# Moving three small buffers, and multiplying constants in four kinds of TensorE waits of the RWKV mixer

## The chip, the cores and the metric

The kernel runs on one core of a Trainium2 chip. The metric is the device time in microseconds (us) of one execution; a run's time is a little longer than the span of the instructions in its profile. TensorE (PE in the profile) multiplies, VectorE (DVE), ScalarE (ACT) and GpSimd (POOL) do the element-wise work, SyncE (SP) issues transfers. The profile also gives TensorE's granted clock, where 1.00 is 2.4 GHz and 0.50 is 1.2 GHz.

## The reference

A backbone of two layers over 256 latent and 256 context tokens of 1024 channels, all in float32. In each layer the modulated rows go through one input projection, which feeds four mixers of 4 heads x 64 channels; their outputs are joined, projected, normed and fed to a gated MLP. The mixer that matters here is RWKV-7, a recurrence over tokens that runs in both directions:

```python
def step(S, xt):
    r_t, w_t, k_t, v_t, a_t, b_t = xt
    sa = jnp.einsum('bhvk,bhk->bhv', S, a_t)
    S = S * w_t[:, :, None, :] + sa[..., None] * b_t[:, :, None, :] + v_t[..., None] * k_t[:, :, None, :]
    return S, jnp.einsum('bhvk,bhk->bhv', S, r_t)
...
for layer in range(DEPTH):
    ...
    y_a = _rwkv7_mixer(...)
    ...
    h = _norm(DEEPNORM_ALPHA * h + mod[2] * y, ln_g[layer, 0], ln_b[layer, 0])
    f = _conv_ffn(_modulate(h, mod[3], mod[4]), ffn_w_up[layer], ...)
```

## The kernel before

The kernel keeps the whole stream in SBUF, channels or tokens on the 128 partitions, and streams the weights in. Each layer is a row of stages, each one a block in which every engine has its own written-out program and waits on semaphores: the input projection with the differential attention, mLSTM, HGRN2, then RWKV (`rwkv`, line 1876, the fourth mixer to be finished), then output projection and MLP (`project_and_feed`). Large float32 products are done as three products of rounded halves (`product`, lines 235 to 237), so weights and rows are split first by ScalarE (line 224) and VectorE (line 228).

SBUF buffers are laid out in the order in which they are made: `const`, `par`, `pr` (34 tiles of 512 columns, and under the name `pr_r` the same memory), `mix` (8 tiles), `modc`, `fcol`, `fold`, `ln2`, `hx`. `pr`, `mix` and `ring` receive weights by transfers; `ring` lies behind `hx`.

The RWKV stage turns the recurrence into products over 4 tiles of 128 tokens (TILES = 4), for direction d = 0 and then d = 1. TensorE's program, in order:

- `turns` (line 1978): transposes of the scaled rows.
- `raw` (line 2022): products of all token pairs of a tile, for the list RAW0. `js` are the tiles whose output is needed: four in layer 0, two in layer 1, so RAW0 has 8 entries in layer 0 and 6 in layer 1. VectorE masks them (`raw_out`, line 2364), GpSimd picks small blocks (line 2277), VectorE reduces them to `diag` (line 2399).
- `solve(d)` (line 2054): 7 products that spread `diag`. VectorE then inverts 8x8 blocks row by row (lines 2413 and 2414) and lays them out (line 2422, semaphore xT). For d = 0 solve(0) comes after the sixth entry of RAW0.
- the loop over j with x0 (line 2074), which waits for xT; then the units u = 0 to 15 with `first` (lines 2089 and 2092) and `second` (lines 2111, 2113 and 2118), which double the size of the inverted blocks, with a copy by ScalarE (line 2596) and one by VectorE (line 2455 or 2461) between them.
- in d = 0, after units 11, 13 and 15 (TURN_AT), the turns for direction 1. The first waits for the semaphore scaled, which VectorE sets at the end of `prepare` (lines 2311 to 2340).
- products P and Q (lines 2145 to 2161), and then the four steps m over the tiles: state products (line 2195), for which VectorE waits (line 2488, semaphore u), and `into_state` (line 2185, semaphore s_mm), for which VectorE waits in line 2504; it then sets s, for which the next step waits.
- in d = 0 solve(1), then the products of y (lines 2228 to 2235).

A helper is there already, and is called with 3 before the first turns and with 2 before the products P of d = 1; its result is read by nobody:

```python
def keep_busy(n, out):
    for _ in range(n):
        nc.tensor.matmul(out, ident, const[:, 0:out.shape[-1]], start=True, stop=True)
```

Of the kernel before, what the change touches and what calls it, by code (L numbers as in the profile page):

```python
# [25 lines left out]
KD = D // P  # L26
SIDE = 256
T = 2 * SIDE
TILES = T // P
# [115 lines left out]
def build(nc, A, out):  # L145
    Stage.zeroed, Stage.made = [], 0
    with ExitStack() as ctx, ExitStack() as between:
        def sb(name, cols):
            return ctx.enter_context(nc.sbuf_tensor(name, [P, cols], F32))

        const = sb("const", N_CONST)
        par = sb("par", N_PAR)
        with nc.sbuf_tensor("pr_r", [P, IN_TILES * T], F32R) as pr_r:
            pass
        pr = sb("pr", IN_TILES * T)
        with nc.sbuf_tensor("mix_r", [P, KD * T], F32R) as mix_r:
            pass
        mix = sb("mix", KD * T)
        modc = sb("modc", DEPTH * 4 * KD * 2)
        fcol = sb("fcol", 16)  # L160
        fold = sb("fold", 2 * KD)
        ln2 = sb("ln2", 2 * KD)
        hx = sb("hx", 2 * D)
        ps = [ctx.enter_context(nc.psum_tensor(f"ps{i}", [P, 512], F32)) for i in range(8)]

        def c(o, n=P, rows=P):
            return const[0:rows, o:o + n]

        ident = c(C_ID)
        stored = ctx.enter_context(nc.semaphore("stored"))  # L170
        E = dict(stored=stored, nc=nc, A=A, out=out, c=c, const=const, ident=ident, par=par, hx=hx, pr=pr, pr_r=pr_r, mix=mix, mix_r=mix_r,
                 modc=modc, fcol=fcol, fold=fold, ln2=ln2, ps=ps)
        for layer in range(DEPTH):
            kept = ExitStack()
            with nc.sbuf_tensor(f"hr0_in{layer}", [P, KD * T], F32R) as hr0, nc.sbuf_tensor(f"hr1_in{layer}", [P, KD * T], F32R) as hr1, \
                    nc.sbuf_tensor(f"wr_in{layer}", [P, 4 * W_IN], F32R) as E["wr"], nc.sbuf_tensor(f"coef{layer}", [P, 20], F32) as E["coef"]:
                E["hr"] = (hr0, hr1)
                with Stage(nc, spans=True) as shared:
                    E["proj"] = Projection(E, shared, layer)
                    if layer == 0:  # L180
                        with nc.sbuf_tensor("hc_in", [P, 2 * D], F32, side="right") as E["hc"]:
                            front(E, layer)
                    else:
                        front(E, layer)
                        between.close()
                    with nc.sbuf_tensor(f"work_in{layer}", [P, 9600], F32) as E["work"]:
                        diff_attention(E, layer)
                    E["cond"] = kept.enter_context(nc.sbuf_tensor(f"cond{layer}", [P, 4 * KD + 32 * KD], F32, side="right"))
                    E["cum"] = hx if layer == 0 else kept.enter_context(nc.sbuf_tensor(f"cum{layer}", [P, 4 * T], F32, side="right"))
                    with nc.sbuf_tensor(f"work_m{layer}", [P, 9600 if layer == 0 else 7952], F32) as E["work"]:  # L190
                        mlstm(E, layer)
            with nc.sbuf_tensor(f"gate_r{layer}", [P, 2 * len(sides(layer)) * D], F32R) as E["gate_r"]:
                pass
            with nc.sbuf_tensor(f"gate{layer}", [P, 2 * len(sides(layer)) * D], F32) as E["gate"]:
                with nc.sbuf_tensor(f"work_r{layer}", [P, 13312], F32R) as E["work_r"], \
                        nc.sbuf_tensor(f"ring_r{layer}", [P, 4096], F32R) as E["ring_r"]:
                    pass
                with nc.sbuf_tensor(f"work{layer}", [P, 13312], F32) as E["work"], \
                        nc.sbuf_tensor(f"ring{layer}", [P, 4096], F32) as E["ring"]:
                    hgrn(E, layer)  # L200
                    with Stage(nc, spans=True) as E["out_sems"]:
                        rwkv(E, layer)
                        kept.close()
                        if layer == 0:
                            E["hc"] = between.enter_context(nc.sbuf_tensor("hc", [P, 2 * D], F32, side="right"))
                        project_and_feed(E, layer)
# [1669 lines left out]
def rwkv(E, layer):  # L1876
# [74 lines left out]
    with Stage(nc) as S, nc.Block() as block:  # L1951
        for n in ("link", "tT", "raw", "raw_out", "masks", "t1", "t1_out", "x_up", "d_mm", "u_mm", "s_mm", "u", "s"):
            S(n)
        fcol = E["fcol"]
# [47 lines left out]
        def _(pe):  # L2002
# [45 lines left out]
            pe.wait_ge(S("tT_out"), 2)  # L2048
            def solve(d):

                pe.wait_ge(S("pick"), 1)
                pe.wait_ge(S("diag"), TILES * (d + 1))
                for n, (s_, _) in enumerate(step_rows(d)):
                    mm = nc.tensor.matmul(spread_row(n), pick[:, s_ * P:(s_ + 1) * P], diag, start=True, stop=True)
                mm.then_inc(S("spread"), 1)
# [9 lines left out]
            for d in range(2):  # L2065
                alT, beT, kT, U, rr_ = alTs[d], beTs[d], kTs[d], Us[d], rrs[d]

                for j in range(TILES):
                    pe.wait_ge(S("xT"), TILES * d + j + 1)
                    if j >= 2:  # L2070
                        pe.wait_ge(S("x_up"), (NU + TILES) * d + j - 1)
                    for hd in range(HEADS):
                        for h in range(2):
                            mm = nc.tensor.matmul(ps[2 + j % 2][rows_of(h), hd * HALF:(hd + 1) * HALF], small(j, 0, hd)[rows_of(h)],
                                                     ident[rows_of(h), rows_of(h)], start=True, stop=True)
                    mm.then_inc(S("x0"), 1)
# [44 lines left out]
                for u in range(NU + 1):  # L2121
                    if u < NU:
                        first(u)
                    if u >= 1:
                        second(u - 1)
                    if d == 1 and u in RAW_AT:
                        raw_next(TILES + RAW_AT.index(u))
                    if d == 0 and u in TURN_AT:
                        r = TURN_AT.index(u)
                        if r == 0:  # L2130
                            pe.wait_ge(S("scaled"), 2)
                        else:
                            pe.wait_ge(S("turned1_out"), r)
                        turns((al, be, ks)[r], (6, 7)).then_inc(S("turned1"), 1)
# [45 lines left out]
                def into_state(j, lh, rh, first_):  # L2180

                    for i in range(2):
                        for q in range(2):
                            a = j * 256 + (2 * i + q) * HD
                            mm = nc.tensor.matmul(ps[2][q * HD:(q + 1) * HD, i * HD:(i + 1) * HD], lh[:, a:a + HD], rh[:, a:a + HD],
                                                  start=first_ and i == 0, stop=not first_ and i == 1)
                    return mm

                pe.wait_ge(S("q_a"), d + 1)
                for m, j in enumerate(ORDER[d]):  # L2190
                    if m:
                        pe.wait_ge(S("s"), (TILES - 1) * d + m)
                        for i in range(2):
                            for q in range(2):
                                mm = nc.tensor.matmul(ps[q][:, i * HD:(i + 1) * HD], PT[q * HD:(q + 1) * HD, i * T + j * P:i * T + (j + 1) * P],
                                                      st[q * HD:(q + 1) * HD, (2 * j + i) * HD:(2 * j + i + 1) * HD], start=True, stop=True)
                        mm.then_inc(S("u_mm"), 1)
                    if m < TILES - 1:
                        into_state(j, kT, vT, True)
                    if d == 0 and m == 1:  # L2200
                        raw_next(3)
                    if d and m in (1, 2):
                        gate(m - 1, True)
                    if d and m == 3:
                        bonus_sum(1)
                    if m:
                        pe.wait_ge(S("u"), (TILES - 1) * d + m)
                    if m < TILES - 1:
                        into_state(j, beT, U if m else Q, False).then_inc(S("s_mm"), 1)
                    if d == 0 and m == 0:  # L2210
                        raw_next(2)
                    if d and m < 2:
                        gate(m, False)
                    if d and m == 2:
                        pe.wait_ge(S("q_b"), 2)
                        bonus_sum(0)
# [1131 lines left out]
```

## Time and profile before

| | |
|---|---|
| median of 3 runs | 1829.49 us (1824.72 to 1830.16) |
| the profiled execution | 1827.64 us |
| its span | 1825.7 us |
| mean granted clock | 0.931 |
| TensorE, VectorE, ScalarE, GpSimd busy | 1636.0, 1090.6, 637.4, 82.9 us |

Busy time of TensorE is the union of its multiplies, whose ends are modelled; a busy TensorE at half the clock does half the work. The share of the whole span says little of a stage of some 100 us, so the rows below are taken from the RWKV stages alone.

### The profile page before, as it was taken

What the parts mean: (1) busy time and instruction counts of PE and PEld (TensorE: products, weight loads), DVE (VectorE), ACT (ScalarE), POOL (GpSimd) and SP (SyncE); (2) the same over time, 40 slices, a digit from 0 to 9 for tenths busy, and PEclk for the clock granted to TensorE, in tenths of its full rate; (3) what the DMA queues carried; (4) which work ended last, traced back from release to release, by engine and by line L of the source; (5) the groups of instructions that cost most, each with busy time, mean ns of one, the idle gap of its engine ahead of it and who ended that gap; (6) DMA issues with size and microseconds to landing.
All of it is one profiled execution on the core that took longest, in us unless ns stands there. A gap on an engine that the chain in (4) does not pass through costs nothing. (4 is left out here: it accounts for less than half of the span.)

```text
span 1825.7 us, 29434 instructions
## 1 busy us (share of the span) xinstructions
PE 1636.0 (90%) x12112; PEld 1284.3 (70%) x12112; DVE 1090.6 (60%) x1870; ACT 637.4 (35%) x1060; POOL 82.9 (5%) x112
## 2 busy tenths in 40 slices
PE   6999999789778999999999979999977688989996
PEld 4766767565477778888877757678754487668875
DVE  2285346885775674554442254735786757578765
ACT  4254221433321245222232242433344231356651
POOL 0000011300201000000000000000120200000000
PEclk8999899899788999999999989999979698989998
DMA  9311111265201034222222022212232201245550
GB/s 391 124 46 47 58 58 58 92 232 186 94 3 48 25 139 154 100 92 93 92 93 92 1 85 81 70 47 81 70 119 92 94 3 48 97 185 188 188 197 23
DMA packets 41620, 182.01 MB, mean 100 GB/s; under 512 B 4752, under 2 KB 5520, under 8 KB 33680
## 3 DMA queue, kind: packets, MB, share of 16 engines
q1 hardware_dynamic: 41488, 180.14, 27.7%
q8 instruction: 96, 1.57, 0.4%
q14 instruction: 36, 0.29, 0.0%
HBM read 179.08 MB, written 1.05 MB: 99 GB/s over the span
## 5 line engine op out<-in xcount | busy, mean ns | idle before, releaser
L235 PE MATMUL ps<-hr_in,wr_in 128*128 128x512 f32 (+1 forms) x544 | 222.0, 408 | 14.4 <-DVE wr_in L228 12.3
L236 PE MATMUL ps<-hr_in,wr_in 128*128 128x512 f32 (+1 forms) x544 | 209.0, 384 | 0.0
L237 PE MATMUL ps<-hr_in,wr_in 128*128 128x512 f32 (+1 forms) x544 | 208.6, 383 | 0.0
L235 PEld LDWEIGHTS ps<-hr_in,wr_in 128*128 128x128 f32 x544 | 108.6, 200 | 65.4 <-issue 36.5
L228 DVE TENSOR_TENSOR wr_in<-mix,wr_in 128x1024 fp32r<-128x1024 f32 x68 | 83.9, 1235 | 93.9 <-ACT wr_in L224 93.5
L235 PE MATMUL ps<-mix_r,work_r 128*128 128x512 f32 (+1 forms) x352 | 136.3, 387 | 1.6 <-DVE work_r L228 1.6
L236 PE MATMUL ps<-work_r 128*128 128x512 f32 (+1 forms) x356 | 135.6, 381 | 0.0
L228 DVE TENSOR_TENSOR work_r<-pr,work_r 128x2048 fp32r<-128x2048 f32 x38 | 87.0, 2289 | 72.1 <-ACT work_r L224 68.0
L237 PE MATMUL ps<-mix_r,work_r 128*128 128x512 f32 x320 | 127.2, 397 | 0.0
L2907 PE MATMUL ps<-mix_r,work_r 128*128 128x512 f32 x336 | 120.7, 401 | 2.3 <-DVE mix_r L228 2.3
L237 PEld LDWEIGHTS ps<-hr_in,wr_in 128*128 128x128 f32 x544 | 108.2, 199 | 19.8
L236 PEld LDWEIGHTS ps<-hr_in,wr_in 128*128 128x128 f32 x544 | 108.7, 200 | 15.4 <-issue 0.2
L224 ACT CAST wr_in<-mix 128x1024 fp32r<-128x1024 f32 x68 | 71.3, 1050 | 109.7 <-PE ps L237 106.0
L224 ACT CAST work_r<-pr 128x2048 fp32r<-128x2048 f32 x40 | 75.8, 1894 | 73.9 <-PEq L2979 68.6
L235 PE MATMUL ps<-work_r,mix_r 128*128 128x512 f32 x232 | 93.3, 402 | 9.0 <-PE ps L237 5.0
L236 PE MATMUL ps<-work_r,mix_r 128*128 128x512 f32 x232 | 93.3, 402 | 0.0
L3203 ACT ACTIVATE pr<-work 128x512 f32<-128x512 f32 (+1 forms) x44 | 23.1, 525 | 199.5 <-DVE work L3069 199.5
L2908 PE MATMUL ps<-mix_r,work_r 128*128 128x256 f32 x320 | 90.2, 282 | 0.0
L236 PEld LDWEIGHTS ps<-work_r 128*128 128x128 f32 x356 | 66.6, 187 | 15.5
L235 PEld LDWEIGHTS ps<-mix_r,work_r 128*128 128x128 f32 x352 | 66.1, 188 | 15.4 <-DVE work_r L228 2.0
L2907 PEld LDWEIGHTS ps<-mix_r,work_r 128*128 128x128 f32 x336 | 64.1, 191 | 18.1 <-issue 2.6
L228 DVE TENSOR_TENSOR work_r<-ring,work_r 128x2048 fp32r<-128x2048 f32 x24 | 54.9, 2289 | 34.5 <-ACT work_r L224 32.1
(503 smaller groups left out, 3364.2 us busy)
## 6 DMA issues: line engine op xcount, KB each, us to landing
mix<-in_w_in SPq DMA_DIRECT2D x68, 512.0 KB, 3.6
pr<-in_w_up SPq DMA_DIRECT2D x28, 1024.0 KB, 4.9
pr<-in_ada_w SPq DMA_DIRECT2D x44, 512.0 KB, 6.3
ring<-in_w_up SPq DMA_DIRECT2D x16, 1024.0 KB, 4.8
ring<-in_ada_w SPq DMA_DIRECT2D x28, 512.0 KB, 4.4
pr<-in_w_down SPq DMA_DIRECT2D x14, 1024.0 KB, 4.9
pr<-in_ada_w SPq DMA_DIRECT2D x8, 1024.0 KB, 15.7
work<-in_w_out SPq DMA_DIRECT2D x16, 512.0 KB, 3.7
```

What stands on the lines that cost most here:

```text
L224: return nc.scalar.copy(high, raw)
L228: return nc.vector.tensor_tensor(low, raw, high.bitcast(F32), ALU.subtract)
L235: nc.tensor.matmul(out, sh, mh, start=first, stop=False)
L236: nc.tensor.matmul(out, sh, ml, start=False, stop=False)
L237: return nc.tensor.matmul(out, sl, mh, start=False, stop=last)
L2907: nc.tensor.matmul(up_bank(f, v)[:, :], sh, hr[0][:, k * T:(k + 1) * T], start=k == 0, stop=False)
L2908: mm = nc.tensor.matmul(up_bank(f, v)[:, SIDE:], sl, hr[0][:, k * T + SIDE:(k + 1) * T], start=False, stop=k == KD - 1)
L3203: nc.scalar.activation(pr[:, f * T + lo0:(f + 1) * T], tb[:, (f % 2) * T + lo0:(f % 2 + 1) * T], ACT.Gelu_apprx_tanh).then_inc(S("gelu"), 1)
```

## The change

Three small buffers, fcol, fold and ln2 (48 columns, 192 bytes in each partition), are made ahead of `pr` instead of behind `modc`. `pr`, `mix` and `modc` so begin 192 bytes later; `hx` and what lies behind it stays in place. And TensorE calls `keep_busy` at four more kinds of places in the RWKV stage, into PSUM banks that nobody needs at that time: (A) 2 multiplies at the head of solve(0), (B) 4 ahead of the x0 loop of d = 0, with a wait for raw_out, only where RAW0 has six entries, which is layer 1, (C) 3 ahead of the first turn for direction 1, and (D) 2 after `into_state` of steps m = 1 and m = 2 of d = 0.

```diff
         par = sb("par", N_PAR)
+        fcol = sb("fcol", 16)
+        fold = sb("fold", 2 * KD)
+        ln2 = sb("ln2", 2 * KD)
...
         modc = sb("modc", DEPTH * 4 * KD * 2)
-        fcol = sb("fcol", 16)
-        fold = sb("fold", 2 * KD)
-        ln2 = sb("ln2", 2 * KD)
...
             def solve(d):
 
+                if d == 0:
+                    keep_busy(2, ps[2][:, :])
                 pe.wait_ge(S("pick"), 1)
...
+                if d == 0 and len(RAW0) == TILES + 2:
+                    pe.wait_ge(S("raw_out"), TILES)
+                    keep_busy(4, ps[0][:, :])
                 for j in range(TILES):
                     pe.wait_ge(S("xT"), TILES * d + j + 1)
...
                         if r == 0:
+                            keep_busy(3, ps[6][:, :])
                             pe.wait_ge(S("scaled"), 2)
...
                         into_state(j, beT, U if m else Q, False).then_inc(S("s_mm"), 1)
+                    if d == 0 and m in (1, 2):
+                        keep_busy(2, ps[0][:, :])
```

## Rows read from the trace of the kernel before

**Rows 1.** The page, busy time and share of the span by engine.

```profile
PE 1636.0 (90%) x12112; PEld 1284.3 (70%) x12112; DVE 1090.6 (60%) x1870; ACT 637.4 (35%) x1060; POOL 82.9 (5%) x112
```

**Rows 2.** Stretches: from:to, length, busy by engine, then granted clock, DMA share, GB/s.

```profile
499.40:501.90 2.50, 0.09 (x3) 0.04 (x1) 2.50 (x5) 0.00 (x0) 1.10 (x1) 1.00 0.00 0
501.90:504.30 2.40, 2.40 (x16) 2.18 (x16) 1.17 (x3) 0.00 (x0) 0.00 (x0) 0.71 0.00 0
...
524.00:534.50 10.50, 9.72 (x320) 9.49 (x320) 8.16 (x10) 4.67 (x12) 0.00 (x0) 1.00 0.01 3
...
538.20:543.30 5.10, 5.10 (x64) 4.77 (x64) 1.64 (x3) 1.69 (x4) 0.00 (x0) 0.50 0.01 3
...
1486.00:1489.20 3.20, 3.20 (x56) 3.08 (x55) 1.09 (x3) 1.81 (x4) 0.00 (x0) 0.50 0.00 0
554.70:567.70 13.00, 11.27 (x161) 10.22 (x160) 8.96 (x20) 1.17 (x2) 4.08 (x4) 1.00 0.01 1
567.70:577.70 10.00, 6.38 (x42) 5.96 (x42) 5.78 (x18) 0.00 (x0) 2.17 (x7) 0.50 0.00 1
```

**Rows 3.** Timeline: start, length, engine, line, what, count, idle before and its end.

```profile
483.60 3.93 PE L2011 MATMUL ps<-const 128*128 128x512 f32 x6
...
610.46 1.98 PE L2011 MATMUL ps<-const 128*128 128x512 f32 x4
...
613.52 1.97 PE L2145 MATMUL ps<-pr,work 128*64 128x128 f32 x32 [1.08 <-DVE pr L2461]
```

**Rows 4.** Timeline around solve(0) and the x0 loop, both layers, and solve(1).

```profile
501.89 2.42 PE L2054 MATMUL ps<-diag,pick 128*128 128x128 f32 x14 [2.41 <-DVE diag L2399]
...
1450.68 2.32 PE L2054 MATMUL ps<-diag,pick 128*128 128x128 f32 x14 [2.37 <-DVE diag L2399]
...
1458.43 3.68 PE L2074 MATMUL ps<-const,pr 64*64 64x64 f32 x64 [5.43 <-DVE pr L2422]
...
1517.98 3.33 PE L2054 MATMUL ps<-diag,pick 128*128 128x128 f32 x14 [1.28 <-DVE diag L2399]
```

**Rows 5.** Timeline around the turns for direction 1, then units of direction 1.

```profile
538.17 1.97 PE L1978 MATMUL ps<-const,ring 128*128 128x128 f32 x8 [3.63 <-DVE work L2340]
...
543.43 1.27 PE L1978 MATMUL ps<-const,ring 128*128 128x128 f32 x8
...
1484.71 1.09 PE L1978 MATMUL ps<-const,ring 128*128 128x128 f32 x8 [3.63 <-DVE work L2340]
...
1488.95 1.26 PE L1978 MATMUL ps<-const,ring 128*128 128x128 f32 x8
...
1547.74 0.27 PE L2092 MATMUL ps<-pr 64*64 64x64 f32 x1
...
1549.37 0.27 PE L2092 MATMUL ps<-pr 64*64 64x64 f32 x1
```

**Rows 6.** Timeline of layer 0 in steps m = 1 to 3 and behind.

```profile
565.57 0.66 PE L2195 MATMUL ps<-st,pr 64*128 64x64 f32 x8 [1.05 <-DVE st L2504]
...
566.75 0.47 DVE L2488 TENSOR_TENSOR work<-work,ps 128x128 f32<-128x128 f32 x2
...
570.09 1.12 PE L2195 MATMUL ps<-st,pr 64*128 64x64 f32 x8 [2.35 <-DVE st L2504]
...
575.74 0.70 PE L2228 MATMUL ps<-pr,work 128*64 128x128 f32 x4
...
582.12 2.34 PE L2074 MATMUL ps<-const,pr 64*64 64x64 f32 x64
```

**Rows 7.** The page: splits of weights, and transfers with their time to landing.

```profile
L228 DVE TENSOR_TENSOR work_r<-pr,work_r 128x2048 fp32r<-128x2048 f32 x38 | 87.0, 2289 | 72.1 <-ACT work_r L224 68.0
...
L228 DVE TENSOR_TENSOR work_r<-ring,work_r 128x2048 fp32r<-128x2048 f32 x24 | 54.9, 2289 | 34.5 <-ACT work_r L224 32.1
...
pr<-in_w_up SPq DMA_DIRECT2D x28, 1024.0 KB, 4.9
...
ring<-in_w_up SPq DMA_DIRECT2D x16, 1024.0 KB, 4.8
```

## The prediction

> **What bounds the kernel now.** I read the page's busy times first. TensorE is busy for 90% of the span [rows 1], so the reader should ask two things of any stretch: does TensorE wait there, and at which clock does it run. I then asked for the stages of the fourth mixer, which runs once in each layer, with the granted clock of each [rows 2]. There TensorE, VectorE and ScalarE hand small pieces to each other, and the clock tells more than the busy share: 1.00 in 524 to 534.5 us, 0.50 from 538.2 to 543.3 and again from 567.7 to 577.7. A granted clock of 0.50 is the 1.2 GHz level, 1.00 the 2.4 GHz one. Each fall follows a wait of TensorE, and the work behind the wait runs at half speed. Last I read the timeline around each wait that the diff touches, for its length, what ended it, and who waits for the work behind it [rows 3 to 6]. Two layers pass the same code, so most rows have a twin: times near 500 are layer 0, near 1450 layer 1.
>
> **What a multiply of constants costs.** The kernel already has such multiplies (line 2011). One multiply shows as two records; two multiplies (4 records) took 1.98 us at full clock, and the work 1.08 us of waiting later, at 613.52, ran in 1.97 us for 32 records, full speed [rows 3]. So two cost 1.98 us, three 2.97 and four 3.96 (multiples of the row). At the low clock they would cost twice that.
>
> **Part A, two multiplies ahead of solve(0), both layers.** TensorE waits 2.41 us for VectorE's diag in layer 0 and 2.37 in layer 1 [rows 4]. Two multiplies (1.98) fit, and start at granted 1.00 [rows 2]; nothing is pushed. If the wait outlasts them and the clock had fallen, they would be late by at most twice 1.98 less 2.41. Behind the wait the 14 records of line 2054 took 2.42 and 2.32 us with the clock falling in them, against 3.33 us for the same 14 with the clock low throughout. Half of that, 1.67, is my estimate for full clock. Gain: 0.75 + 0.65 = 1.40 us. VectorE's line 2413 waits for exactly this, and VectorE then solves and lays the rows out alone, one after another, so the gain stays. After the multiplies only 0.4 us of waiting is left; I take all of it.
>
> **Part B, four multiplies ahead of the x0 loop, layer 1 only.** The condition holds only where RAW0 has six entries, so layer 0 (eight) is unchanged there. The added wait on raw_out for four is met long before, and asks nothing new. The wait is 5.43 us; four multiplies fill 3.96 of it. Behind it 64 records of line 2074 took 3.68 us [rows 4], against 2.34 us for 64 in the second direction at full clock [rows 6]: ceiling 1.34 us. But some 1.5 us of waiting is left, a second if part A ends sooner, and the trace's waits of 2.4 us are followed by a fall. The floor is nothing. Between the ends I take half, 0.67.
>
> **Part C, three multiplies ahead of the first turn to direction 1, both layers.** The wait for VectorE is 3.63 us in both layers [rows 5], three multiplies are 2.97, so 0.66 is spare. What they cover in layer 0: eight transposes 1.97 against 1.09 us in layer 1 (0.88); from their end at 540.14 to the next turn at 543.43 is 3.29 us, and the same two rounds of units without a fall, in direction 1 of layer 1, took 1549.37 - 1547.74 = 1.63, about half (1.66 saved); next turn 1.27 against 1.09 (0.18). Together 2.72. In layer 1 the first turn was already fast: 1485.80 to 1488.95 is 3.15 (1.52 saved), the next turn 1.26 (0.17), together 1.69. Ceiling 4.41, floor 0. Little waiting is left and dense work follows, but ScalarE's copies of the turned rows may become the next to wait for, so I take 3.8.
>
> **Part D, two multiplies in steps m = 1 and 2 of direction 0, both layers.** In m = 1 the wait is only 1.05 us [rows 6], so 1.98 makes TensorE 0.93 late. Queued behind it are the state products (line 2195) for which VectorE's line 2488 waits; but that one starts at 566.75, while the products ended at 566.23, because VectorE is in line 2364. This covers 0.52, so at most 0.41 us is lost in each layer, and nothing if the tail of the last record overlaps. I take 0.3, 0.6 for both. In m = 2 the wait is 2.35, and 1.98 fits. What it buys: the products of m = 3 took 1.12 against 0.66 us (0.46); the 14 records of solve(1) took 3.33, half of it saved (1.66); VectorE's second solve, and through it direction 1, starts only after them. In layer 0 the products of y follow on TensorE, from 575.74 to the records of line 2074 at 582.12, longer than VectorE needs; the part of them at the low clock, to 577.7, is 1.96 us, half of it saved (0.98). In layer 1 the y products are fewer and VectorE ends last, so this third piece counts nothing there. Sum: 3.10 + 2.12 = 5.22, floor 0. After the multiplies two waits of 0.4 and 1.3 us are left close to each other, so the clock may still fall inside solve(1). I take three quarters, 3.9.
>
> **Part E, the moved buffers.** fcol, fold and ln2 take 48 columns of four bytes; pr, mix and modc begin 192 bytes later, hx and everything behind it stays. What this could change is how fast engines or transfers reach pr and mix. The trace has a comparison: by the sizes of the buffers, pr lies 320 bytes off ring counted modulo 512, and splitting 128x2048 from either took 2289 ns in both, 1 MB into either landed in 4.9 and 4.8 us [rows 7]. I take 0. No row shows the new offset, so a loss or gain can't be excluded, only called unlikely.
>
> **The sum.** 1.40 + 0.67 + 3.8 + 3.9 - 0.6 = 9.2 us. With every ceiling it is 1.40 + 1.34 + 4.41 + 5.22 = 12.4, less 0.6: 11.8. Behind the mixer nothing has a time of its own: the loads of w_out wait for the mixer's own y and buffers, so the gain is not eaten by a transfer. The profiled execution took 1827.64 (span 1825.7, 1.94 around it), which becomes 1818.4; it lies 1.85 under the median of 1829.49, so against the median I forecast 1820.3.
>
> **Rivals.**
> *The clock falls anyway.* The multiplies only put the fall off; what gains is what stands right behind them: part A 1.40, the first turn of layer 0 0.88, the products of m = 3 0.92, less 0.6, together 2.6 us: 1826.9. For it: at 1.00 the kernel fell after waits of 2.4 us [rows 2, 4], and part B and D leave 1.5 to 2. Against it: the pair at 610.46 held the clock over 1.08 us [rows 3]. Chance 0.25.
> *The transposes don't hold it.* In C the clock could fall after the turn, though the multiplies carried it there, because eight transposes follow. Then C gives 0.88 and the time is 1829.5 - 6.3 = 1823.2. For it: layer 1's clock stood at 0.50 from 1486 on, just behind a turn that had run at full speed [rows 2, 5]. Against: it had waited 3.63 before. Chance 0.10. The Trainium skill has this rule (TensorE: Matmul & The Clock Gate, Part 4: PE-mode transpose): a transpose "doesn't count as PE-busy the same way". By it the sum would be 6.3 where my reading of the rows gives 9.2; that transposes run at either level the trace does show (1.97 and 1.09 us for eight), whether they count it doesn't.
> *Slower: the multiplies themselves run at the low clock.* Two then cost 3.96 us: A 1.55 late, D 2.39 and 1.61, C (5.94) 2.31, in each layer, and B 2.49: 2 x 7.86 + 2.49 = 18.2 us, with no gain: 1847.7. It decides from where two multiplies take longer than the 2.35 to 2.41 us of A and D. Against it: granted 1.00 stands in the stretches in front of A, C and D [rows 2]; for it: the three at 483.60 took 3.93 because they began low [rows 3]. Chance 0.07.
> *The new addresses matter.* Either sign, unpriced by any row: 0.03.
>
> **Chances and range.** The forecast itself has 0.55, with its own range 1817.7 (all ceilings) to 1824 (a little over half). A difference of 0.3%, about 5.5 us, is what a measurement of this kernel can tell from none (the three runs spread over 5.4). Faster by more: most of the forecast, half of the transpose rival: 0.60. Within: the fall anyway and the weaker part of the others: 0.32. Slower: 0.08. The range reaches from 1816.5 to 1829, which leaves out the slow rival and little else.
>
> **What would show it.** In the profile after: 22 more multiplies (A 4, B 4, C 6, D 8), as 44 records beside the 20 of line 2011. A right: line 2054 near 1.7 us in solve(0). B right: line 2074 in layer 1 near 2.4. C right: clock 1.00 over the turn and the next two rounds, 1.6 instead of 3.3 us. D right: line 2195 of m = 3 at 0.66, line 2054 of solve(1) near 1.7, and line 2488 of m = 2 no more than 0.4 late. E right: means of lines 228 and 235 to 237 unchanged. I am wrong if the clock row shows 0.50 behind the same waits, or if a wait's work now starts later than before.

## The result, and the profile after

| | before | after |
|---|---|---|
| median | 1829.83 us (1824.72 to 1832.50) | 1803.27 us (1801.06 to 1804.96, 4 runs) |
| ratio | | 0.9875 [0.9855, 0.9896] |
| span of the profiled execution | 1825.7 us | 1799.2 us |
| mean granted clock | 0.931 | 0.946 |

The change takes 1.25% off by the ratio, 19 to 27 us by its interval (the two medians alone lie 26.6 us apart, at the interval's edge), where 9.2 were forecast. TensorE's busy time falls by 13 us though it has 44 records more, against [rows 1]; VectorE's is the same to 0.1%:

```profile
PE 1622.9 (90%) x12156; PEld 1273.7 (71%) x12156; DVE 1089.7 (61%) x1870; ACT 637.9 (35%) x1060; POOL 82.8 (5%) x112
```

**The RWKV stages.** Stretches of after, in the columns of [rows 2]: the products of solve(0), the wait for scaled, the turns and rounds behind it, the products ahead of the steps with m = 0 and 1, and the steps m = 2 and 3 with solve(1) and the y products. All stand at 1.00, where [rows 2] has 0.71 at solve(0), 0.50 behind the first turn and 0.50 from the step m = 3 on:

```profile
491.70:493.40 1.70, 1.70 (x14) 1.59 (x14) 1.17 (x3) 0.00 (x0) 0.00 (x0) 1.00 0.00 0
...
524.30:527.80 3.50, 2.63 (x7) 0.84 (x6) 3.40 (x4) 0.00 (x0) 0.00 (x0) 1.00 0.01 2
527.80:534.30 6.50, 5.86 (x105) 5.23 (x105) 4.30 (x11) 3.32 (x8) 0.00 (x0) 1.00 0.01 3
538.50:551.80 13.30, 13.30 (x168) 12.64 (x168) 6.41 (x13) 2.25 (x4) 2.89 (x3) 1.00 0.01 1
...
553.80:566.40 12.60, 11.02 (x139) 8.69 (x140) 9.86 (x32) 0.00 (x0) 2.94 (x7) 1.00 0.01 2
```

The timeline of after, in the columns of [rows 3 to 6]. In the order of the parts: solve(0) (A), the x0 loop of layer 1 (B), the first two turns (C), steps m = 1 to 3 and solve(1) (D), and the x0 loop and the first units of direction 1 behind them:

```profile
491.69 1.80 PE L2056 MATMUL ps<-diag,pick 128*128 128x128 f32 x14 [0.46 <-DVE diag L2407]
...
1429.41 3.60 PE L2011 MATMUL ps<-const 128*128 128x512 f32 x8
1435.00 2.39 PE L2079 MATMUL ps<-const,pr 64*64 64x64 f32 x64 [2.00 <-DVE pr L2430]
...
527.76 1.09 PE L1978 MATMUL ps<-const,ring 128*128 128x128 f32 x8 [0.87 <-DVE work L2348]
...
531.01 1.09 PE L1978 MATMUL ps<-const,ring 128*128 128x128 f32 x8 [0.22 <-ACT work L2612]
...
551.84 1.98 PE L2011 MATMUL ps<-const 128*128 128x512 f32 x4
553.76 0.66 PE L2201 MATMUL ps<-st,pr 64*128 64x64 f32 x8
...
554.47 0.48 DVE L2496 TENSOR_TENSOR work<-work,ps 128x128 f32<-128x128 f32 x2 [0.23 <-PE ps L2201]
...
555.39 1.98 PE L2011 MATMUL ps<-const 128*128 128x512 f32 x4
557.48 0.66 PE L2201 MATMUL ps<-st,pr 64*128 64x64 f32 x8
559.41 1.80 PE L2056 MATMUL ps<-diag,pick 128*128 128x128 f32 x14 [1.27 <-DVE diag L2407]
...
566.45 2.34 PE L2079 MATMUL ps<-const,pr 64*64 64x64 f32 x64
...
574.88 1.00 PE L2022 MATMUL ps<-work,ring 64*128 64x128 f32 x5 [1.75 <-issue]
575.81 1.12 PE L2094 MATMUL ps<-pr 64*64 64x64 f32 x16
```

These waits are filled as meant, and the work behind them runs at full speed: 1.80 us where [rows 4] had 2.42 and 3.33, 1.09 where [rows 5] had 1.97, 0.66 where [rows 6] had 1.12. The last two rows are something new: TensorE stands for 1.75 us and nothing that the profile shows releases it ("issue"), and the 16 products behind it take 1.12 us.

To see what each piece is worth I measured from the start of one VectorE instruction to the start of a later one, the same two in each trace, in us:

| stretch | layer 0 before | after | layer 1 before | after |
|---|---|---|---|---|
| start of the stage to the first row of the inversion (A) | 14.49 | 13.82 | 13.99 | 13.78 |
| rows laid out, to the first copy of the units (B in layer 1) | 4.82 | 5.21 | 5.40 | 4.08 |
| last line of `prepare` to the next copy of the units (C) | 5.67 | 3.77 | 4.66 | 3.78 |
| on to the steps (C) | 10.54 | 10.26 | 10.54 | 10.26 |
| steps m = 0 and 1 (D) | 13.63 | 13.94 | 13.63 | 13.94 |
| to the inversion for direction 1 (D) | 9.16 | 6.85 | 9.16 | 6.86 |
| inversion to the end of the layout (D) | 6.42 | 5.34 | 5.02 | 5.02 |
| first units of direction 1 | 9.00 | 12.01 | 8.44 | 11.15 |
| the whole stage | 141.80 | 138.92 | 133.09 | 131.28 |

So the two stages give 4.7 us together, after giving back 5.7 in the first units of direction 1. Two rows need care. The start of layer 0's stage (A) scatters by itself: in the kernels below that have no new multiply it takes 13.60 to 14.59 us, so the 0.67 us there is within the scatter (in layer 1 those take 13.86 to 14.45 and the ones with multiplies 13.47 to 13.78). And layer 0's x0 loop, which has no multiplies, takes 0.39 us more: TensorE waits 3.80 us there, and the clock stands at 0.50 from 499.8 to 506.6.

**Outside the RWKV stages.** The same measure over the whole kernel finds the larger part in the MLP, where no line was changed. From VectorE's instruction at 730.16 to the one at 931.76, the up projection of layer 0, before takes 201.60 us and after 195.84. The next stretch (to 1049.12) falls from 117.36 to 115.42, the last one of layer 1 (1770.89 to VectorE's last instruction) from 48.22 to 46.01. These are 9.9 us. The last of the three is partly the clock's: in before TensorE's clock stood at 0.50 for 5.5 us of it, in after for 2.5, and of two kernels below that keep the MLP slow one takes 46.07 us there (move_128) and one 46.68 (modc_ahead). The product groups of TensorE, grouped by line and tile in 760 to 900 us, columns as on the page: count, busy time, mean of one. Before:

```profile
L237 PE MATMUL ps<-mix_r,work_r 128*128 128x512 f32 x201 | 79.9, 397 | 0.0
L235 PE MATMUL ps<-mix_r,work_r 128*128 128x512 f32 x200 | 79.4, 397 | 0.0
L236 PE MATMUL ps<-work_r 128*128 128x512 f32 x200 | 78.2, 391 | 0.0
```

and after:

```profile
L236 PE MATMUL ps<-work_r 128*128 128x512 f32 x207 | 80.5, 389 | 0.0
L237 PE MATMUL ps<-mix_r,work_r 128*128 128x512 f32 x207 | 80.5, 389 | 0.0
L235 PE MATMUL ps<-mix_r,work_r 128*128 128x512 f32 x206 | 80.1, 389 | 0.0
```

The reader is to see the counts, not the busy times: in the same 140 us at granted 1.00 TensorE starts 601 products before and 620 after, one in 232.9 ns against one in 225.8 (140 us over the count, so good to one product; a single product overlaps the next). The weights, both halves, are the stationary operand and lie in `work_r`; the high half of the rows that move through lies in `mix_r`, their low half in `work_r`. `mix` is one of the buffers that moved. In the timeline of before the three lines start 235, 228 and 237 ns after one another, in that of after 227, 227 and 226.

Of the 26.5 us between the two profiles 10.2 remain ahead of layer 0's RWKV stage, which starts at 490.3 us before and at 480.1 after. There the granted clock scatters: later profiles with the layout of after start that stage at 481.1, 482.7, 487.8 and 490.4 us, those with before's at 488.7 and 490.3. The mean clock up to there is 0.92 before and 0.94 after, and 0.92 x 490.3 and 0.94 x 480.1 are both 451 us of full clock: by this the 10.2 us are the clock's, and the profile of after was a lucky one. I count nothing of it for either part.

### The profile page after: what moved, and what is told of

It is laid out like the page before. It is cut to its first block and busy times, and to the rows that moved or that the text cites. A ratio compares the mean times of both kernels' runs of the same rounds, so it can differ in the third digit from the quotient of the medians.

```text
span 1799.2 us, 29522 instructions
## 1 busy us (share of the span) xinstructions
PE 1622.9 (90%) x12156; PEld 1273.7 (71%) x12156; DVE 1089.7 (61%) x1870; ACT 637.9 (35%) x1060; POOL 82.8 (5%) x112
## 5 line engine op out<-in xcount | busy, mean ns | idle before, releaser
L228 DVE TENSOR_TENSOR work_r<-pr,work_r 128x2048 fp32r<-128x2048 f32 x38 | 86.9, 2288 | 71.1 <-ACT work_r L224 67.0
L228 DVE TENSOR_TENSOR work_r<-ring,work_r 128x2048 fp32r<-128x2048 f32 x24 | 54.9, 2288 | 34.1 <-ACT work_r L224 31.6
```

The source lines that it names most:

```text
L228: return nc.vector.tensor_tensor(low, raw, high.bitcast(F32), ALU.subtract)
```

## Experiments

**Each part alone.** *move_only* has the three lines of the buffers and no new multiply, *multiplies_only* the multiplies and the buffers in their old place. move_only:

```diff
         par = sb("par", N_PAR)
+        fcol = sb("fcol", 16)
+        fold = sb("fold", 2 * KD)
+        ln2 = sb("ln2", 2 * KD)
...
-        fcol = sb("fcol", 16)
-        fold = sb("fold", 2 * KD)
-        ln2 = sb("ln2", 2 * KD)
```

> Only the three small buffers are moved; no multiplies of constants are added. Theory 1 (the two reads of TensorE, the stationary rows and the moving rows, disturb each other by where they lie relative to each other): the step from product to product in the MLP falls from 235/228/237 ns to about 227 as in the changed kernel, and most of the time is here: 14 to 22 us faster (1808 to 1816). Rival (the multiplies keep the clock up in the whole kernel, the buffers do nothing): 0 to 2 us, and steps of 235/228/237 ns stay.

Measured: 1813.59 us against 1824.94, ratio 0.9937 [0.9917, 0.9957], at a clock (0.934) that is nearly before's. The step between products came out as expected, the size did not: 11 us where 14 to 22 were expected. The up projection takes 195.84 us, the same as after to the hundredth. The whole page has these means for its two product groups, where the profile of before has 387 and 397:

```profile
L235 PE MATMUL ps<-mix_r,work_r 128*128 128x512 f32 (+1 forms) x352 | 133.8, 380 | 1.6 <-DVE work_r L228 1.6
L237 PE MATMUL ps<-mix_r,work_r 128*128 128x512 f32 x320 | 124.5, 389 | 0.0
```

multiplies_only:

```diff
             def solve(d):
 
+                if d == 0:
+                    keep_busy(2, ps[2][:, :])
...
+                if d == 0 and len(RAW0) == TILES + 2:
+                    pe.wait_ge(S("raw_out"), TILES)
+                    keep_busy(4, ps[0][:, :])
...
+                            keep_busy(3, ps[6][:, :])
...
+                    if d == 0 and m in (1, 2):
+                        keep_busy(2, ps[0][:, :])
```

> All four kinds of multiplies, buffers where they were. Theory 1: 5 to 11 us faster (1819 to 1825), with line 235 to 237 as before; this is what the prediction put down. Rival (multiplies do it all): 24 to 28 us faster.

Measured: 1816.22 us, ratio 0.9949 [0.9929, 0.9970], clock 0.946; the up projection stays at 201.60. The product of the two ratios is 0.9886, inside the interval of the whole change: the parts add. The move is the larger half by the ratios, but their intervals overlap.

**Which distance, and whose.** Counted modulo 512 bytes, pr and mix begin at 416 before and work, ring, hx and wr at 96; after, all are at 96. Four kernels ask whether the place itself or the distance counts. *move_64* moves only fcol ahead (pr, mix and modc 64 bytes later), *move_128* fcol and fold (128 bytes):

```diff
         par = sb("par", N_PAR)
+        fcol = sb("fcol", 16)
...
-        fcol = sb("fcol", 16)
```

> Only fcol (64 bytes) ahead of pr: pr, mix and modc 64 bytes later, fold and ln2 stay, hx stays. Counted modulo 128, mix then lies as work does; modulo 256 it does not (128 off). If the relation counts modulo 128: steps of 227 ns, as fast as move_only. If it counts modulo 256 or 512: some other steps, 0 to half of the gain. If any later start helps: a third of the gain.

> fcol and fold (128 bytes) ahead of pr: pr and mix 128 bytes later, 192 bytes off work counted modulo 256. If the relation counts modulo 256 or 128: steps of 233 to 237 ns as before or others, no gain or a small one, not two thirds of it. If any later start helps: two thirds of the gain.

Measured: move_64 1819.96 us, ratio 0.9974 [0.9957, 0.9990]; move_128 1824.61, ratio 0.9984 [0.9966, 1.0003]. The product groups of move_64 lie between the two, with 613 starts in 140 us:

```profile
L235 PE MATMUL ps<-mix_r,work_r 128*128 128x512 f32 x205 | 80.6, 393 | 0.0
L237 PE MATMUL ps<-mix_r,work_r 128*128 128x512 f32 x204 | 79.8, 391 | 0.0
L236 PE MATMUL ps<-work_r 128*128 128x512 f32 x204 | 79.2, 388 | 0.0
```

and those of move_128 are as slow as before's, with 598:

```profile
L236 PE MATMUL ps<-work_r 128*128 128x512 f32 x200 | 79.7, 399 | 0.0
L235 PE MATMUL ps<-mix_r,work_r 128*128 128x512 f32 x199 | 79.1, 398 | 0.0
L237 PE MATMUL ps<-mix_r,work_r 128*128 128x512 f32 x199 | 78.1, 392 | 0.0
```

So it is not "the later the better". (By their times alone move_64, move_128 and modc_ahead below, at 0.9974, 0.9984 and 0.9981, can't be told apart; their order rests on these stretches.) Nor does the distance modulo 128 bytes suffice: by it move_64 would be as after, which has 620 starts and not 613.

*small_right* leaves pr and mix where they were and takes the three small buffers out of the row to the far end of SBUF, so that hx, wr, gate, work and ring begin 192 bytes earlier: all the large buffers are then at 416, none at 96.

```diff
-        fcol = sb("fcol", 16)
-        fold = sb("fold", 2 * KD)
-        ln2 = sb("ln2", 2 * KD)
+        fcol, fold, ln2 = (ctx.enter_context(nc.sbuf_tensor(name, [P, 16], F32, side="right")) for name in ("fcol", "fold", "ln2"))
```

> No multiplies are added. fcol, fold and ln2 are made at the other end of the memory: pr and mix stay where they were, and hx, hr, wr, gate, work and ring begin 192 bytes earlier. Counted modulo 512, pr, mix and work then lie alike (416). Theory 1 (what counts is the place of the stationary rows relative to the moving rows): steps of 226 to 227 ns in the MLP of layer 0, 195.84 us for the stretch of it that took 201.60, and as fast as move_only, 0.992 to 0.996. Rival (the absolute place of pr and mix counts): 235/228/237 ns and no gain.

Measured: 1813.64 us, ratio 0.9923 [0.9906, 0.9940], the up projection again 195.84. Its groups (the lines are two numbers lower):

```profile
L233 PE MATMUL ps<-mix_r,work_r 128*128 128x512 f32 x207 | 80.5, 389 | 0.0
L234 PE MATMUL ps<-work_r 128*128 128x512 f32 x206 | 80.1, 389 | 0.0
L235 PE MATMUL ps<-mix_r,work_r 128*128 128x512 f32 x206 | 80.1, 389 | 0.0
```

That settles it for the relative place: `pr` and `mix`, which moved in after, didn't move here, and the gain is the same.

*modc_ahead* moves pr and mix by 512 bytes, which leaves every distance as it was modulo 512:

```diff
         par = sb("par", N_PAR)
+        modc = sb("modc", DEPTH * 4 * KD * 2)
...
-        modc = sb("modc", DEPTH * 4 * KD * 2)
```

> No multiplies are added. Only modc (512 bytes) is made ahead of pr, so pr and mix begin 512 bytes later, the small buffers and hx stay. Modulo 512 the relation is that of before. Theory 1: steps of 235/228/237 ns and no gain (ratio 0.997 to 1.003). Rival (any later start helps, or a distance below 512 bytes): a gain of about 0.6%.

Measured: 1824.83 us, ratio 0.9981 [0.9962, 0.9999], the up projection 201.60. A move as such gives nothing there. The sum of three steps is before's, but not each step: the three lines start 233, 236 and 231 ns after one another here, against 235, 228 and 237.

*mix_later* puts the small buffers between pr and mix, so only mix and modc move:

```diff
         pr = sb("pr", IN_TILES * T)
+        fcol = sb("fcol", 16)
+        fold = sb("fold", 2 * KD)
+        ln2 = sb("ln2", 2 * KD)
...
         mix = sb("mix", KD * T)
         modc = sb("modc", DEPTH * 4 * KD * 2)
-        fcol = sb("fcol", 16)
-        fold = sb("fold", 2 * KD)
-        ln2 = sb("ln2", 2 * KD)
```

> No multiplies are added. The small buffers are made between pr and mix: mix and modc begin 192 bytes later, pr stays. Theory 1 with mix alone (mix_r holds the rows of both halves of the MLP, work_r the weights): all of move_only's gain in the MLP, 195.84 us again, and only the few products of pr_r with ring_r keep steps of 229 to 232 ns. If pr counts too (weights are split out of it): part of the gain only.

Measured: 1813.36 us, ratio 0.9941 [0.9916, 0.9966], the up projection 195.84. Of the two large buffers that moved, `mix`, which holds the modulated rows of the MLP, brings nearly all of it.

The up projection by distance (pr and mix less work, modulo 512; the stretch is as many products in each, 864 by 201.60 us over the 233.3 ns of before's three starts):

| distance | kernels | stretch, us | per product, ns |
|---|---|---|---|
| 320 | before, modc_ahead, multiplies_only | 201.60 | 233.3 |
| 384 | move_64 | 197.76 | 228.9 |
| 448 | move_128 | 202.56 | 234.4 |
| 0 | after, move_only, small_right, mix_later | 195.84 | 226.7 |

No run tells 512 bytes from 256 as the period: the four distances are 64, 128, 192 and 0 modulo 256, and the moves by 512 bytes fit both.

**Where the multiplies' gain is given back.** The four first transfers of w_out are issued just ahead of direction 1 (SyncE's line 1999 in after). They run densely up to the moment in which TensorE stands still. Stretches of after, the last three numbers being clock, DMA share, GB/s: the products ahead of the stall, the stall, and the products behind it:

```profile
569.50:573.10 3.60, 3.60 (x99) 3.23 (x94) 1.46 (x3) 0.91 (x3) 0.00 (x0) 1.00 1.03 393
573.10:574.90 1.80, 0.05 (x3) 0.03 (x2) 1.11 (x2) 0.00 (x0) 0.00 (x0) 0.99 0.23 84
...
574.90:578.40 3.50, 3.50 (x55) 3.27 (x57) 0.00 (x0) 0.37 (x1) 0.00 (x0) 0.52 0.03 8
```

and its twin in layer 1, from the timeline:

```profile
1505.28 0.44 PE L2123 MATMUL ps<-pr 64*64 64x64 f32 x6 [1.84 <-issue]
...
1506.74 1.12 PE L2094 MATMUL ps<-pr 64*64 64x64 f32 x16
```

In before the same spot had 0.40 and 0.46 us of "issue", behind transfers at 0.86 of the engines and 325 GB/s. (In layer 1 of after the stall begins 5.4 to 6.8 us behind the four issues, later than the expectation below says.) *loads_later* is after with each of the four transfers held back until a few units of direction 1 are done:

```diff
             for n in range(KD):
+                if n < EARLY:
+                    sp.wait_ge(S("x_up"), NU + 2 * TILES + 4 + 2 * n)
                 if n >= EARLY:
```

> The changed kernel, with the first four loads of w_out issued one by one behind units 4, 6, 8 and 10 of direction 1 instead of all at the y products. In the changed kernel TensorE stood still for 1.84 us in layer 1, 1.5 to 3 us after these loads were issued, with nothing that the profile shows as a reason. Theory 2 (its instructions arrive late because the loads fill the transfer engines): the stand shrinks below 0.5 us in both layers, the clock stays up behind it in layer 1, and the stretch from line 2442 to the first unit's line 2455 falls from 12.0 and 11.2 to 8.5 to 9 us; 3 to 6 us faster than the changed kernel (ratio 0.984 to 0.986). Rival (another cause, such as a fetch at that place whatever is loading): the stand remains, same time as the changed kernel.

Measured: 1800.29 us (1798.07 to 1808.58), ratio 0.9861 [0.9840, 0.9882]. In time alone that can't be told from after, but the profile is plain. The same units now run without a stop, and the loads come later and thinner, 0.43 to 0.45 of the engines in layer 0 instead of 1.03 (0.43 to 0.62 in layer 1). Layer 0:

```profile
573.03 1.16 PE L2024 MATMUL ps<-work,ring 64*128 64x128 f32 x16
574.12 0.68 PE L2096 MATMUL ps<-pr 64*64 64x64 f32 x16
574.64 0.63 PE L2118 MATMUL ps<-pr 64*64 64x64 f32 x16
```

```profile
582.00:586.00 4.00, 4.00 (x118) 3.81 (x116) 3.81 (x7) 0.71 (x3) 0.00 (x0) 1.00 0.43 138
```

The first units of direction 1 take 8.39 and 7.78 us where after took 12.01 and 11.15 and before 9.00 and 8.44. So the stall goes with the four loads at that place; loads_later changes both their moment and their density, and doesn't tell which counts.

The traces say more of what TensorE lacks. They have a transfer queue named "instruction", whose packets are 16 KB. One of them moves around the start of the stall in layer 0 of after (packets, MB and share of the 16 engines in 573 to 575 us):

```profile
q8 instruction: 1, 0.02, 1.5%
```

Counted from VectorE's first instruction of the stretch "first units of direction 1", layer 0 and layer 1:

| | TensorE stops | the packet lands | TensorE goes on |
|---|---|---|---|
| before | 7.19, 6.82 | 6.15, 5.83 | 7.59, 7.27 |
| after | 6.47, 4.88 | 6.86, 5.39 | 8.22, 6.72 |
| multiplies_only | 6.47, 4.88 | 6.34, 5.76 | 7.94, 7.27 |
| loads_later | never | 3.74, 2.75 | |

All kernels follow this. Those without the new multiplies stop at 7.19 and 6.82 us, if they stop. All 16 stalls over 0.25 us, in eight kernels, end 1.3 to 1.6 us after the landing of the packet. modc_ahead, whose packets land first of those with the loads at that place (5.91 and 5.70), has no such stall, and the three kernels with later loads, where they land by 3.74, have none. So TensorE comes to a fixed place of its program and stands there until a packet of instructions, late behind the loads, is in. The new multiplies make the stall longer because the stop comes 0.7 and 1.9 us sooner. This is read from the traces, not tested: no run moves that packet alone, the trace doesn't say whose instructions it holds, and why the place shifts by just this much is open.

**Part B with six multiplies.** *six_ahead* is loads_later with

```diff
-                    keep_busy(4, ps[0][:, :])
+                    keep_busy(6, ps[0][:, :])
```

> As the kernel with the later loads, with six instead of four multiplies ahead of the x0 loop of layer 1. With four, TensorE still waited 2.00 us behind them and the 64 records of the x0 loop took 2.39 us in one profile and 3.21 in another. Theory (that rest of the wait lets the clock fall): with six the rest is about 0.3 us and the 64 records take 2.3 to 2.4 us, about 1 us faster than the later loads alone where the clock fell there; too little to show in the times, so the ratio stays 0.985 to 0.987. Rival (six last longer than the wait): the records start later, nothing gained.

Measured: 1794.09 us (1793.04 to 1799.49) against 1823.35, ratio 0.9851 [0.9822, 0.9880], clock 0.950: the best version here, though its lead over loads_later (0.9861) is within the intervals. The x0 loop in layer 1 of loads_later (two lines lower than after):

```profile
1429.05 3.60 PE L2013 MATMUL ps<-const 128*128 128x512 f32 x8
1434.65 3.21 PE L2081 MATMUL ps<-const,pr 64*64 64x64 f32 x64 [2.00 <-DVE pr L2432]
1437.63 1.63 PE L2096 MATMUL ps<-pr 64*64 64x64 f32 x32
```

and of six_ahead:

```profile
1427.71 5.32 PE L2013 MATMUL ps<-const 128*128 128x512 f32 x12
1433.32 2.39 PE L2081 MATMUL ps<-const,pr 64*64 64x64 f32 x64 [0.29 <-DVE pr L2432]
1435.52 1.13 PE L2096 MATMUL ps<-pr 64*64 64x64 f32 x32
```

With four, 2.00 us of waiting are left, and the loop behind them ran once at full clock (after, 2.39) and three times not (3.21 in loads_later, 3.22 in multiplies_only and one_step, whose VectorE stretches are 5.29, 5.30 and 5.29 us). With six 0.29 is left and the loop is fast: 1.2 us of VectorE's time from there to the next step (4.08 against 5.29). One profile shows it for six, and with four one in four was as fast, so that six does it each time is likely and not shown.

**Part D without its first step.** *one_step* is loads_later with

```diff
-                    if d == 0 and m in (1, 2):
+                    if d == 0 and m == 2:
```

> As the kernel with the later loads, with the two multiplies of direction 0 only in step m = 2 and not in m = 1. If those of m = 2 are enough: VectorE's stretch from line 2472 to line 2488 of m = 2 falls from 13.94 to 13.63 us, and the next, to the second solve, stays 6.86. If m = 1 is needed for the clock: the next stretch goes back to 7.5 to 9.2 us, more than the 0.3 us that it saves.

A single time, 1804.12 us, clock 0.937. The lateness of m = 1 is gone, 13.63 us again for 13.94, but the next stretch is 7.18 for 6.86 in layer 0 and 7.76 in layer 1: 20.81 and 21.39 us together, where loads_later has 20.80 in both. At m = 1 the two multiplies pay for themselves in one layer and bring 0.6 us in the other. The 14 products of solve(1) take 1.80 us in layer 0 here too, full speed; in layer 1 the clock falls within them, behind a wait of 1.27 us, and they take 2.39 (this stretch of one_step holds them):

```profile
1498.00:1501.00 3.00, 2.47 (x16) 2.28 (x18) 0.51 (x2) 0.00 (x0) 0.00 (x0) 0.76 0.00 0
```

So the pair of m = 2 is enough in one layer and not in the other. The single time, 3.8 us above loads_later's median, is within the scatter of loads_later's own times (to 1808.58), and I draw nothing from it.

## Why the prediction was wrong

**The step that failed is part E,** "I take 0". The comparison made there, splits of weights from pr and ring, holds: line 228 takes 2288 ns for 128x2048 in after and 2289 in [rows 7]. It compared VectorE and the transfers, though, and never asked the third reader of these buffers, which is busy for 90% of the time. The trace of before had a sign of it: the three products of the MLP, with `mix_r` and `work_r` 320 bytes apart modulo 512, start every 233.3 ns on average, none of them in the stretch above under 228, while products with both buffers at equal places often start every 226 or 227: `work_r` with `gate_r` in 40 steps of 47, `hr_in` with `wr_in` in 601 of 1065 (mean 229.0). The move is worth 0.63% [0.43, 0.83], 11 us. The rival "new addresses matter" named it and gave it 0.03 without a price, and the check for it, "means of lines 228 and 235 to 237 unchanged", is where it shows: 228 is unchanged, 235 and 237 are 7 and 8 ns shorter on the page of move_only.

The Trainium skill has a rule here that the runs limit (TensorE: Matmul & The Clock Gate, Part 2: What happens when you issue a matmul): the array has "two independent SBUF read ports", so that loading the next weights doesn't take bandwidth from the running product. By it alone one would expect no distance to matter. The measured step changes by 7.8 ns (6.72 us over 864 products) with the distance alone, so the stream of row and weight reads is not free of their relative place. Whether they meet in the memory, and where, no run here shows.

**Parts A to D** came out at the forecast sum, partly by luck: their terms were off in both directions. In the terms of the prediction, with VectorE's stretches as the measure:

| part | forecast | measured |
|---|---|---|
| A | 1.40 | 0.6 to 1.2 (0.37 to 0.67 in layer 0, 0.21 to 0.52 in layer 1) |
| B | 0.67 | 0.1 or 1.3, as the clock falls in the wait of 2.00 or not |
| C | 3.8 | 3.3 (1.90 + 0.28 in layer 0, 0.88 + 0.28 in layer 1) |
| D | 3.9 | 5.7 (2.30 in each layer, 1.08 for the y products) |
| lateness of m = 1 | -0.6 | -0.62 |
| given back | 0 | -1.2 to -3.6 in each layer |

The price of the multiplies was a little high: three take 2.84 us, four 3.60 and six 5.32, not multiples of 0.99, so that more of each wait was left than counted. A is smaller because the 14 products take 1.80 us at full clock and not the 1.67 that half of 3.33 gave: 0.62 and 0.52 on TensorE. In C the ceiling of 4.41 was counted on TensorE; the rounds behind the first turn wait for ScalarE's copies (0.22 and 0.42 us in after), so VectorE sees less of it. D reached past its ceiling of 5.22: the clock did not fall in the waits of 0.1 and 1.27 us left, and the terms themselves measure 2.30 for 2.12 in each layer and 1.08 for 0.98. The gain that was said to stay, "nothing has a time of its own" behind the mixer, was partly lost earlier: to the stall under the first w_out transfers. They were taken for something that waits, and not for something that disturbs. Taken together A to D are 9.1 to 10.9 us by this table, less what is given back, and multiplies_only measures 9.3 us (0.51%) with an interval from 5.5 to 13, which holds the forecast and the 5.9 us that its two stages show.

**The rivals.** *The clock falls anyway* is refuted for A, C and D by clock 1.00 in the stretches above, and half true for B. *The transposes don't hold it* is refuted: the clock is 1.00 from 527.8 to 534.3 us, with both turns at 1.09. The rule cited for it (the Trainium skill, TensorE: Matmul & The Clock Gate, Part 4: PE-mode transpose) is neither borne out nor refuted by this: a turn of eight transposes lasts 1.09 us and has other products around it. *Slower* did not occur: two multiplies took 1.98 or 1.99 us wherever they were put.

## What to carry to other kernels

Where one matmul loop takes most of the time, measure start to start of its products for every pair of buffers in it, and compare pairs: a few ns in each are a per cent of the kernel. If they differ, the places of the stationary and the moving buffer modulo 512 bytes (or 256, which these runs don't tell apart) are the first thing to look at, and moving any small buffer between them is a free trial. Multiplies of constants in a wait pay when they leave little of it, and are not lost if they leave a step 0.3 us late; look then at what the earlier work runs into, here a place at which TensorE stands while loads fill the transfer engines.

## What the hardware showed that was not expected

- Three float32 products of 512 columns with equal places modulo 512 start every 226.7 ns on average. At distances of 320, 384 and 448 bytes it is 233.3, 228.9 and 234.4. A period of 256 bytes would fit as well. Both absolute places tried (96 and 416) are equally fast if they are the same for both buffers.
- TensorE stood for 1.75 and 1.84 us, with nothing to wait for that the profile shows, right behind transfers at 0.90 and 1.03 of the DMA engines; with the transfers later and at 0.43 to 0.62 it did not. In before, at 0.86, it was 0.40. Each such stall ended 1.3 to 1.6 us after a 16 KB packet of the queue named "instruction" had landed.
- A wait of 2.00 us behind four multiplies let the clock fall in three profiles of four. A wait of 1.27 behind two did not let it fall in after, in either layer, where two more stood ahead; in layer 1 of one_step, without those two, it did.
